# A one-core backbone step: first norm by output halves on VectorE alone, experts chosen by pairwise comparisons, slot table by rounded one-hot products

## What is computed

```python
out = (ga * y_a + gb * y_f + gc * y_p) @ w_out               # token mixer, 640 x 1024
x   = layer_norm(ALPHA * x + gate1 * out) * ln1_g + ln1_b     # the first norm
u2  = x * (1 + scale2) + shift2
p_group = softmax(u2 @ w_r1 + b_r1);  g_val, g = top_1(p_group)      # 4 groups
fine    = (u2 @ w_r2 + b_r2)[g];      e_val, e = top_2(fine)         # 4 experts of that group
e_w     = softmax(e_val) * g_val
y = sum over the token's two experts of e_w * down(silu(up_a(u2)) * up_b(u2))   # 16 experts
x = layer_norm(ALPHA * x + gate2 * y) * ln2_g + ln2_b
```

## Time and profile before

| | us |
|---|---|
| median of 3 runs (1033.0 to 1036.87) | 1034.57 |
| the profiled execution | 1032.05 |
| its span | 1030.2 |
| PE busy | 906.6 (88%) |
| DVE busy | 432.1 (42%) |
| ACT busy | 335.7 (33%) |
| POOL busy | 237.2 (23%) |

### The profile page before, as it was taken

The page is one execution under the profiler, slowest core; times in us unless marked ns, Lnnn a source line. Parts: engine busy times, 40 slices in busy tenths (PEclk is TensorE's granted clock), DMA queues, the critical chain, the costliest instruction groups (busy, mean ns, idle before and its releaser), DMA issues.

```text
span 1030.2 us, 22201 instructions
## 1 busy us (share of the span) xinstructions
PE 906.6 (88%) x8752; PEld 651.3 (63%) x8752; DVE 432.1 (42%) x861; ACT 335.7 (33%) x594; POOL 237.2 (23%) x306
## 2 busy tenths in 40 slices
PE   1799889999999999999999979359999999999953
PEld 0398668857777777776676767336656656665521
DVE  3634832004434454651324894642244341243318
ACT  1433302114434342431212210323345453254415
POOL 2276600000100000000000374212434433343340
PEclk9799988999999999998999979559999999999987
DMA  9978645332120301231012511996889999799552
GB/s 317 402 217 298 217 180 200 142 122 83 21 82 1 123 21 62 84 129 75 20 62 90 217 42 47 395 375 230 339 313 411 410 410 393 282 353 411 169 214 102
DMA packets 63946, 207.56 MB, mean 201 GB/s; under 512 B 7550, under 2 KB 7940, under 8 KB 60828
## 3 DMA queue, kind: packets, MB, share of 16 engines
q1 hardware_dynamic: 51536, 175.55, 45.1%
q0 software_dynamic: 8592, 26.39, 7.1%
q10 hardware_dynamic: 3772, 5.00, 1.5%
HBM read 186.96 MB, written 19.96 MB: 201 GB/s over the span
## 4 chain that ended last, share of the span: by engine, by line
PE 69%; DVE 12%; DMA 6%; ACT 6%; issue 3%; POOL 3%; SPq 1%; ACTq 0%; POOLq 0%; DVEq 0%
PE ps L1683 24%; PE ps L1941 15%; PE ps L1600 7%; PE ps L1926 6%; PE ps L1669 3%; DMA ring<-in_w_mod 2%; PE ps L1800 2%; PE ps L1916 2%; PE ps L1737 1%; ACT expert_w L1009 1%; DVE R_x L1224 1%; ACT w_hi L851 1%; POOL R_x L711 1%; PE ps L1973 1%; PE ps L1951 1%
## 5 line engine op out<-in xcount | busy, mean ns | idle before, releaser
L1941 PE MATMUL ps<-expert_w,R_p 128*32 128x256 f32 x3072 | 177.4, 383 | 0.9 <-ACT R_p L1032 0.7
L1941 PEld LDWEIGHTS ps<-expert_w,R_p 128*32 128x32 f32 x3072 | 100.0, 111 | 61.1 <-issue 3.9
L1683 PE MATMUL ps<-w_hi,uT_hi 128*128 128x512 f32 x320 | 134.7, 421 | 4.2 <-ACT R_x L948 2.4
L1683 PE MATMUL ps<-w_lo,uT_hi 128*128 128x512 f32 x320 | 127.8, 399 | 0.0
L1179 DVE TENSOR_TENSOR w_lo<-ring,w_hi 128x1024 fp32r<-128x1024 f32 x52 | 67.3, 1323 | 123.8 <-ACT w_hi L851 123.0
L1926 PE MATMUL ps<-expert_w,R_p 128*32 128x256 f32 x1536 | 91.7, 379 | 0.5 <-ACT R_p L1061 0.5
L1009 ACT COPY expert_w<-staged 128x1024 f32 (+1 forms) x87 | 85.5, 1044 | 19.8 <-PE ps L1941 8.6
L1517 DVE COPY expert_w<-staged 128x1024 f32 x105 | 69.7, 695 | 43.1 <-PE ps L1941 25.7
L1535 DVE TENSOR_TENSOR R_p<-R_p,ps 128x128 f32<-128x128 f32 x48 | 13.8, 287 | 151.6 <-ACT R_p L1051 151.6
L1683 PEld LDWEIGHTS ps<-w_hi,uT_hi 128*128 128x128 f32 x320 | 61.1, 191 | 21.1 <-issue 4.0
L1926 PEld LDWEIGHTS ps<-expert_w,R_p 128*32 128x32 f32 x1536 | 50.1, 110 | 33.3 <-ACT R_p L1061 0.8
(11 more groups left out here) (350 smaller groups left out, 1462.5 us busy)
## 6 DMA issues: line engine op xcount, KB each, us to landing
staged<-in_w_up SPq DMA_DIRECT2D x128, 512.0 KB, 12.1
staged<-in_w_down SPq DMA_DIRECT2D x64, 512.0 KB, 10.8
ring<-in_w_in SPq DMA_DIRECT2D x11, 2048.0 KB, 8.0
R_d<-in_w_mod SPq DMA_DIRECT2D x13, 1024.0 KB, 5.3
ring<-in_w_mod SPq DMA_DIRECT2D x8, 1024.0 KB, 20.5
y_slots<-R_s ACTq DMA_DIRECT2D x1, 4608.0 KB, 18.8
ring<-in_w_out SPq DMA_DIRECT2D x2, 2048.0 KB, 7.9
R_p<-in_w_mod SPq DMA_DIRECT2D x3, 1024.0 KB, 8.0
```

What stands on the lines that cost most here:

```text
L1683: i = mm(out, parts(k)[a][:, tok(j)], w[b][:, k], start=(k == 0 and a + b == 0), stop=(k == KD - 1 and b == 1))
L1941: m = mm(ps[SUB * g:SUB * (g + 1), 0, 0:256].rearrange("p (h n) -> p h n", h=2), xT[:, k % 4, at:at + SUB], up_w[:, k, :, P * g:P * (g + 1 ...
```

## The change

The first norm reads each half of the projection as soon as PE has finished it (`out_half`), with half-row operations for the product, the sum and the statistics. `u2` is made from the un-normalised row: `(r - mean) * scale2` runs while ACT takes the square root (EPS now comes as ACT's bias), then `* rstd + shift2` by halves, each half announced by itself (`u2_half`), and PE's transposes wait for one half only. The two operations for `x`, which POOL did, are now DVE's.

The router's bias becomes one more product of PE (a row of ones times `b_r`) for each tile. The best group and the two best experts come from ranks: for all 25 quadruples of a token row at once, six comparisons write "beaten by" flags, and one sum counts them. The running sums over tiles are left to PE, by five products of the rounded masks `both_r` with a triangle and with ones; the count of each expert is a product of its own behind a second wait. DVE reads both straight from PSUM. The two experts' slots are made in one operation each. The one-hots are written in the rounded format, whose products PE takes in one pass instead of two. The table is read right after the one-hots, ahead of the plan; DVE writes the first index column itself (`idx_now`), and POOL's first gather no longer copies it.

```diff
             for j in range(NT):
-                pool.wait_ge(S["x1_pre"], j + 1)
-                chain(nc_t(x_tok[:, j], resid[j % 2], ROW1["g1"], ALU.mult))
-                nc_t(x_tok[:, j], x_tok[:, j], ROW1["b1"], ALU.add).then_inc(S["x1_ready"], 1)
-                pool.wait_ge(S["u2_ready"], j + 1)
+                pool.wait_ge(S["u2_half"], 2 * j + 2)
                 pool.dma_start(u2_rows[tok(j), :], u2[:, j % 2]).then_inc(S[f"u2_stored{j % 2}"], 16)
...
-                nc.scalar.activation(rstd[:, j:j + 1], rstd[:, j:j + 1], ACT.Sqrt).then_inc(S["r_std"], 1)
+                nc.scalar.activation(rstd[:, j:j + 1], mv[:, 2 * j + 1:2 * j + 2], ACT.Sqrt, bias=eps_col).then_inc(S["r_std"], 1)
...
+                for n in range(2):
+                    if n:
+                        take(dve, ("out", j))
+                    else:
+                        dve.wait_ge(S["out_half"], j + 1)
+                    i = tt(rj[:, half(n)], ps[:, b0 + n, :], ROW1[f"gate1_{c_}"][:, half(n)], ALU.mult)
...
+                    ch(stt(rj[:, half(n)], x_tok[:, j, half(n)], ALPHA, rj[:, half(n)], ALU.mult, ALU.add))
+                    ch(nc.vector.bn_stats(stats[:, 6 * n:6 * n + 6], rj[:, half(n)]), wait=(n == 1))
+                mean, scale = mv[:, 2 * j:2 * j + 1], rstd[:, j:j + 1]
+                nc.vector.bn_aggr(mv[:, 2 * j:2 * j + 2], stats).then_inc(S["r_var"], 1)
...
+                ch(stt(u2[:, j % 2], rj, mean, ROW1[f"scale2_{c_}"], ALU.subtract, ALU.mult), wait=False)
+                dve.wait_ge(S["r_std"], j + 1)
+                ch(nc.vector.reciprocal(scale, scale))
+                for n in range(2):
+                    stt(u2[:, j % 2, half(n)], u2[:, j % 2, half(n)], scale, ROW1[f"shift2_{c_}"][:, half(n)], ALU.mult, ALU.add
+                        ).then_inc(S["u2_half"], 1)
+                ch(stt(rj, rj, mean, ROW1["g1"], ALU.subtract, ALU.mult))
+                stt(x_tok[:, j], rj, scale, ROW1["b1"], ALU.mult, ALU.add).then_inc(S["x1_ready"], 1)
...
+            for d in range(1, EPG):
+                m = EPG - d
+                ch(tt(beaten[:, :, 4 * d:4 * d + 5 * m - 4:5], quads[:, :, 0:m], quads[:, :, d:EPG], ALU.is_ge), wait=False)
+                i = tt(beaten[:, :, d:d + 5 * m - 4:5], quads[:, :, d:EPG], quads[:, :, 0:m], ALU.is_gt)
+                ch(i, wait=(d == EPG - 1))
+            ch(nc.vector.tensor_reduce(ranks.rearrange("p j n -> p (j n)"), R_s[:, 0:400].rearrange("p (n k) -> p n k", k=EPG), AX.X, ALU.add))
+            ch(ts(g_hot, ranks[:, :, 0:NG], 0.5, None, ALU.is_lt))
...
+            stt(both_r.rearrange("p (j g e) -> p j g e", j=NT, g=NG), rank_f, 1.5, of_group, ALU.is_lt, ALU.mult).then_inc(S["masks_ready"], 1)
...
+            ch(tt(prod_two, two, for_both(place), ALU.mult))
+            ch(nc.vector.tensor_reduce(slot.rearrange("p s j -> p (s j)"), prod32, AX.X, ALU.add))
...
+            take(dve, "slots")
+            ts(idx_now[:], bank(1)[:, 0:1], const("half"), None, ALU.add).then_inc(S["idx_col"], 1)
+            release(ts(tile_idx[:, 0:MAXP], bank(1)[:, 0:MAXP], const("half"), None, ALU.add), "slots")
...
-                pe.wait_ge(S["u2_ready"], j + 1)
                 for k in range(2):
+                    pe.wait_ge(S["u2_half"], 2 * j + k + 1)
...
+                lg = bank(1)[:, j * 20:(j + 1) * 20]
+                mm(lg, const("one")[0:1, :].to_broadcast([1, P]), b_r[0:1, :], start=True, stop=False)
...
-            mm(bank(0)[:, 0:NT * NE], const("tri"), both_all, start=True, stop=False)
-            mm(bank(0)[:, 0:NT * NE], ones, before_all[:, 0:NT * NE], start=False, stop=True)
-            i = mm(bank(0)[:, NT * NE:(NT + 1) * NE], ones, before_all[:, NT * NE:], start=True, stop=True)
+            for d in range(NT):
+                mm(bank(0)[:, d * NE:NT * NE], ones_r if d else tri_r, both_r[:, 0:(NT - d) * NE], start=(d == 0), stop=(d == NT - 1))
+            pe.wait_ge(S["masks_ready"], 2)
+            i = mm(bank(0)[:, NT * NE:(NT + 1) * NE], const("one").to_broadcast([P, P]), chosen, start=True, stop=True)
```

More of the change, by code:

```diff
@@ L86, in shape_constants @@
              ("quarter", (4 * (p % SUB) + p // SUB - 4 * SUB)[:, None]),
-             ("one", np.ones((P, 1))), ("zero", np.zeros((P, 1)))]
+             ("one", np.ones((P, 1))), ("zero", np.zeros((P, 1))), ("eps", np.full((P, 1), EPS))]
     at, where = 0, {}
@@ L1382, in _, with half @@
             take(dve, ("yT", H - 1, 0))
+            ch(nc.vector.tensor_copy(tri_r, const("tri")), wait=False)
+            ch(nc.vector.tensor_copy(ones_r, const("one").to_broadcast([P, P])), wait=False)
+            def half(k):
+                return slice(k * BW, (k + 1) * BW)
             for j in range(NT):
@@ L1436, in _ @@
-            tt(route_b, m2, m3, ALU.subtract).then_inc(S["route_sel"], 1)
-            for hot, em in ((hot1, e1), (hot2, e2)):
-                ch(tt(em.rearrange("p j (g e) -> p j g e", g=NG),
-                      g_hot.rearrange("p j (g a) -> p j g a", a=1).to_broadcast([P, NT, NG, EPG]),
-                      hot.rearrange("p j (a e) -> p j a e", a=1).to_broadcast([P, NT, NG, EPG]), ALU.mult))
-            ch(tt(both, e1, e2, ALU.add))
-            ch(nc.vector.memset(before[:, 0], 0.0))
@@ L1445, in _ @@
-            for j in range(NT):
-                i = tt(before[:, j + 1], before[:, j], both[:, j], ALU.add)
-                if j < NT - 1:
-                    ch(i)
-            i.then_inc(S["masks_ready"], 1)
+            for d in range(1, EPG):
[3 more added lines that the diff above has]
+                ch(i, wait=(d == EPG - 1))
@@ new lines, in _ @@
+            dve.wait_ge(S["masks_ready"], 1)
+            nc.vector.tensor_reduce(chosen, both_r.bitcast(F32).rearrange("p (j e) -> p e j", j=NT), AX.X, ALU.add).then_inc(S["masks_ready"], 1)
+            e1, e2 = e12[:, 0:NT], e12[:, NT:]
+            ch(stt(by_expert(e1), rank_f, 0.5, of_group, ALU.is_lt, ALU.mult), wait=False)
+            ch(nc.vector.tensor_reduce(m1, lc, AX.X, ALU.max))
+            ch(tt(e2, both_r.bitcast(F32).rearrange("p (j e) -> p j e", j=NT), e1, ALU.subtract))
+            two = e12.rearrange("p (s j) e -> p s j e", s=2)
@@ L1494, in _ @@
             stt(plan[:, 0:MAXP], change[0:1, 0:LAST:2], 64.0, word, ALU.mult, ALU.add).then_inc(S["plan_ready"], 1)
-            take(dve, "slots")
-            ch(nc.vector.tensor_copy(tile_idx[:, MAXP:], const("half").to_broadcast([P, 2])), wait=False)
-            ch(ts(y_idx[:], const("tiles")[:, 0:LAST + 1], 4.0 * SUB, const("quarter"), ALU.mult, ALU.add), wait=False)
-            release(ts(tile_idx[:, 0:MAXP], bank(1)[:, 0:MAXP], const("half"), None, ALU.add), "slots")
             dve.wait_ge(S["route_exp"], 1)
@@ L1866, in route @@
                     begin(pe, "lg")
-                i = product(bank(1)[:, j * 20:(j + 1) * 20], "lg", lambda k: u2T[:, j % 2, k], lambda k: w_r[:, k], KD)
+                lg = bank(1)[:, j * 20:(j + 1) * 20]
+                mm(lg, const("one")[0:1, :].to_broadcast([1, P]), b_r[0:1, :], start=True, stop=False)
+                for k in range(KD):
+                    i = mm(lg, u2T[:, j % 2, k], w_r[:, k], start=False, stop=(k == KD - 1))
                 if j == NT - 1:
@@ L1881, in _ @@
                 merged_split(d)
-                token_major(bank(4), ("out", 0), ("out", 0), mT_parts, 0, True, False, [d])
+                i = token_major(bank(4), ("out", 0), ("out", 0), mT_parts, 0, True, False, [d])
+            i.then_inc(S["out_half"], 1)
             filled(token_major(bank(5), ("out", 0), ("out", 1), mT_parts, 0, True, False), ("out", 0))
```

133 lines of the change are left out of this document (62 added, 71 removed).

## The result

| | before | after |
|---|---|---|
| median of the runs, us | 1034.54 (1033.0 to 1036.87, 4 runs) | 1015.87 (1014.74 to 1016.82, 4 runs) |
| ratio | | 0.9826 [0.981, 0.9843] |
| profiled execution | 1032.05 | 1015.79 |
| span | 1030.2 | 1014.0 |

The forecast was 1016 (1008 to 1023). The medians differ by 18.7 us, the two profiled executions by 16.3. To see where they come from, I cut each trace at four moments that every kernel here has: R0, when PE has ended tile 2's projection and begins route 0; D, when DVE begins on the last half of tile 4's projection (in experiment 4, where it begins on both only then, on the first); L, DVE's first operation on the logits; M, PE's first expert product.

A forecast was written before the change was run, and what follows sets the result against it. A 105 us relay of DVE, PE, ACT, POOL and one DMA was taken to bound the kernel; 4.2 + 5.1 + 9.0 = 18.3 us off the profiled 1032.05 gives 1013.7, 1016 as median, range 1008 to 1023.

The forecast's parts named there:

- the rival of the weight loads: Expert loop: paced by weight loads, so only their 4.2 us is gained; 1030.4 us, chance 0.04.
- Term 1: Projection and routing of tiles 0 to 3: tile 4's projection ends at 638.05 instead of 642.25; gain 4.2 us.
- the slower rival: First norm: fused operations cost 3.25 us a row even without POOL, a tile 19.4; end at 1046 us, chance 0.03.
- Term 2: From the end of tile 4's projection to the logits: 11.4 us instead of 16.56; gain 5.1 us.
- Term 3: From the logits to the first expert product: 20.5 us instead of 29.45; gain 9.0 us.
- The six comparisons: DVE's ranks behind the logits: 0.8 us for six by the trace row, about 1.4 by the skill's rule.
- the rival of 1009.5: PE's clock stays at 2.4 GHz through both pairs of routes; gain 25.1 us, 1009.5 us, chance 0.25.
- ACT's copies: Copies of expert 0's weights: hidden, ending at 662.4; as rival, the loop waits for them, 1021.5 us, chance 0.12.

The follow-up runs named there:

- experiment 4: Changed kernel, but DVE waits for both halves of the projection before starting on the first; 1017.7 us, ratio 0.9857 to the kernel before.
- experiment 3: Changed kernel, with POOL given four multiplications per tile beside the norm, result unread; 1026.69 us, ratio 0.9927 to the kernel before.
- experiment 8: Changed kernel, with 32 dense products, result unread, where PE waits behind the last router product; 1016.64 us, ratio 0.9844 to the kernel before.
- experiment 1: Kernel before with only the new first norm; choice of experts, counts and slot table as they were; 1025.37 us, ratio 0.9913 to the kernel before.
- experiment 5: Changed kernel, with the reading of the slot table put back behind the plan on DVE; 1020.61 us, ratio 0.9871 to the kernel before.
- experiment 6: Changed kernel, with the slot table's one-hots in plain F32, so each product is two passes; 1019.07 us, ratio 0.9854 to the kernel before.
- Experiment 10: Changed kernel, where each of the six comparisons waits for the one before; 1017.4 us, ratio 0.9848 to the kernel before.
- experiment 7: Changed kernel, with PE's router transposes and products placed singly between dense projection halves; 1012.58 us, ratio 0.98 to the kernel before.
- 11: Kernel of experiment 9 without its 5 dense products; 1010.24 us, ratio 0.9777 to the kernel before.
- experiment 12: Kernel of experiment 9 with 17 more dense products ahead of the first gathered rows' transposes; 1007.09 us, ratio 0.975 to the kernel before.
- experiment 9: Kernel of experiment 7 with transposes 2 and 3 moved earlier and 5 unread dense products ahead of transposes 4; 1005.35 us, ratio 0.9728 to the kernel before.

## Why the prediction was right, point by point

**What bounds the kernel.** The relay of the engines does. Nothing behind M changed (341.94 and 341.57), so the rival of the weight loads is out: had the loads paced the loop, the 17 us would have come back there.

**Term 1**, 4.2 predicted, 3.6 measured. The chain of steps held. Counted from R0, tile 0 ended at -2.4 (forecast 596.9 - 599.37 = -2.5), the folds costing DVE 1.5, 0.78 and 1.05 in three operations where I had put some 1 each; route 1's transposes began at +4.3 (forecast 4.3), tile 3's projection at +10.5 (10.2). The rest of the miss is the projection's slow begin, 13.71 instead of 13.39. The fused row was 1.28, not 1.22, and the slower rival with 3.25 a row is out; experiment 3 shows that POOL's arithmetic is what makes such a row slow (2.31).

**Term 2**, 5.1 predicted, 4.9 measured. D to `u2`'s first half took 4.63, worked out as 4.6; experiment 4 shows 2.0 of this term to be the early half. The fused operations, `u2` in halves and POOL's leaving share the rest; they were not taken apart.

**Term 3**, 9.0 predicted, 8.3 measured, the largest miss. Logits to counts took 4.07 (2.2 + 1.7 predicted), counts to the last one-hot 6.30 (6.4), gather 6.35 (6.45), transposes and copy 2.64 (2.67). The table was there 0.70 after the last one-hot, not 0.4 (0.38 in experiment 8, where the clock was up: my price was one for the other clock), and the gather started 1.13 after DVE began the index column, not 0.70. Here the price was wrong, and its reason: I took POOL's 0.70 from the table's end to the gather and took off 0.25 for the copy that goes, but without the copy it is 0.91. In both kernels with the copy (before and experiment 1) the "issue" ahead of the first gather is 0.17, in the twelve without it 0.54 or 0.55. It doesn't hang on the plan: in experiment 5, where the plan is ready first, it is 0.54 too.

```profile
667.04 1.04 POOL L773 DMA_INDIRECT R_p<-u_rows,idx_now  x1 [0.54 <-issue]
```

Leaving out the copy thus gained nothing; why the issue grows was not tried. By the rows, term 3 is 4.2 from the choice and the counts (8.23 to 4.07), 1.0 up to the last one-hot (7.26 to 6.30), 3.2 from there to the index column (3.90 to 0.70), 0.2 lost ahead of the gather and 0.1 gained in it. The 4.2 of experiment 5 and the 2.1 of experiment 6 do not add up beside these: behind the plan the two-pass products are hidden, as they were before (they ended at 677.1, and the table was read at 678.20), so one pass is worth something only with the table first.

**The six comparisons.** The row said 0.8, and 0.89 was measured up to the reduction. The Trainium skill, "VectorE: DVE Perf Modes", section "The DRAIN you can't avoid", says that leaving out the semaphores saves nothing; the same section also says that a next operation that is not held starts earlier. Experiment 10 goes against the first sentence for operations as small as these (1.68 with semaphores, 0.89 without) and agrees with the second, which the prediction did not weigh.

**The clock.** It fell during route 1 as forecast, so the rival of 1009.5 did not come about. What a held clock is worth was rather underrated: I had 8.3 for the stretch from R0 to D; experiment 7 shows 42.88 - 30.88 = 12.0, of which some 2.3 is product 2, moved behind D. The new order also fills PE's waits, so not all of the rest is the clock. The reason that I gave against the rival (thin work just ahead had not held the clock) stands: in experiments 7 and 11 it was full as long as single thin pieces stood between dense halves, and fell at 635.9 and 633.7, behind the run of thin pieces and waits that begins at 630, each time in a wait or at its end.

**ACT's copies** stayed hidden with 5 us of cover; the last store of `u2` landed early enough. That rival is out.

**The sum.** 18.3 was predicted and 16.8 measured from R0 to M (3.60 + 4.94 + 8.26). With 0.4 behind M, and R0 0.97 later, 16.2 of span are left. That the median still fell on the forecast is partly luck: the profiled execution before lay 2.5 below its median, and I carried this offset over, while the one after lies at its median (1015.79 and 1015.87).

## What to carry to other kernels

In a relay of engines, price every link between two engines by itself and add: here eleven groups of rows gave the gain from R0 to M to within 2 us. A result that another engine waits for (the slot table) goes ahead of work that nobody waits for yet, and the moved work must be short enough for what then covers it. In this kernel thin matmuls kept PE's clock when they stood one by one between dense ones; standing together, with the waits between them, they lost it, and the work behind them paid for it. Whether the waits or the thin work weigh more was not taken apart.

## What the runs showed of the hardware

- The granted clock, and what PE did ahead of it: in experiment 12 it fell just after 635.5, behind 5.5 us of router pieces and 5 dense products with a single wait of 0.33; through product 1 of the changed kernel PE made products of 20 columns without a break for 3.4 us, and the clock stayed at 0.50. With the same kind of pieces between dense halves, and no wait, it was 1.00 for 30 us (experiment 7). The falls before (605.1), after (606.1) and in experiments 7 and 11 came in waits of PE or at their end. Dense products whose result nobody reads gave 4.9 us (experiment 9 against 11), but the same ones let the clock fall earlier in experiment 12.
- A higher clock can cost time: in experiment 12 PE got ahead of the second gather, waited 2.31, and the clock fell in that wait (2.4 us). In experiment 8 a wait of 1.99 left it up.
- DVE and POOL on SBUF rows at the same time: 2.3 instead of 1.28 on DVE for a row, 2 us on POOL for half a row (experiment 3). Half-row products that read PSUM stayed at 0.67 to 0.69 beside POOL's folds.
- Small DVE operations without a wait between them begin 0.11 to 0.16 us apart, although each shows 0.2 to 0.29; with a wait 0.24 to 0.32.
